# Overflow rows of a mixture of experts: from a scatter through memory to a product with a slot-by-token table

## What is computed

```
scores = sigmoid(x @ router_w)            # 16 experts in 4 groups
g_best = the best group; idx = the 2 best experts in it
gates  = scores of these two, divided by their sum
a   = einsum('td,edf->tef', x, w_gate);  up = einsum('td,edf->tef', x, w_up)
mid = silu(a) * up * gates
y   = einsum('tef,efd->td', mid, w_down)
x   = x + gate_vector * y                 # adaLN gate, one vector for prompt, one for sample
```

## Time and profile before

| what | us |
|---|---|
| median of three runs (range) | 875.19 (871.82 to 876.34) |
| the profiled execution | 876.51 |
| its span, first to last instruction | 874.6 |
| PE / DVE / ACT / POOL busy | 791.7 / 359.8 / 284.9 / 109.2 |
| mean granted TensorE clock | 0.965 of 2.4 GHz |

### The profile page before, as it was taken

One profiled execution on the slowest core, in us unless ns is written; L12 is line 12 of the kernel. 1 busy time (PEld: TensorE's weight loads), 2 busy tenths in 40 slices (PEclk: granted clock), 3 DMA queues, 4 the chain that ended last, 5 costly groups with the idle time before them and its releaser, 6 DMA issues.

```text
span 874.6 us, 11923 instructions
## 1 busy us (share of the span) xinstructions
PE 791.7 (91%) x4251; PEld 455.1 (52%) x4251; DVE 359.8 (41%) x837; ACT 284.9 (33%) x663; POOL 109.2 (12%) x155
## 2 busy tenths in 40 slices
PE   7999999999899999999885889999999999999860
PEld 4358755535444566555444536656544575554430
DVE  5770642642463442422115364475632434221115
ACT  1651222201640341222213347677611422221111
POOL 1400000010000011110112021320300111110120
PEclk8999999999899989999998899999999999999995
DMA  8993333299943387999987964320156669999955
GB/s 280 368 346 105 102 103 116 88 348 300 341 170 124 107 319 255 409 410 409 410 326 254 368 234 156 99 65 35 51 173 260 225 196 403 411 410 409 400 200 216
DMA packets 84119, 218.67 MB, mean 250 GB/s; under 512 B 9682, under 2 KB 19547, under 8 KB 83741
## 3 DMA queue, kind: packets, MB, share of 16 engines
q1 hardware_dynamic: 74046, 197.89, 62.1%
q0 software_dynamic: 8512, 16.48, 5.4%
q10 hardware_dynamic: 1504, 3.56, 1.1%
HBM read 213.13 MB, written 14.83 MB: 261 GB/s over the span
## 4 chain that ended last, share of the span: by engine, by line
PE 54%; DMA 11%; SPq 11%; issue 10%; DVE 6%; ACT 3%; POOLq 3%; DVEq 1%; POOL 1%; ACTq 0%
PE ps L980 49%; SPq L722 4%; SPq L692 4%; DMA arena<-in_moe_w_up_dram 3%; PE ps L987 3%; DMA ring<-in_moe_w_down_dram 2%; DMA hT_xn<-y_rows 2%; SPq L675 2%; DMA x<-in_x_sample_dram 2%; SPq L728 1%; DMA mod_rows<-modrow 1%; PE ps L1222 1%; DVEq L2068 1%; POOLq L948 1%; DMA y_rows<-arena,rows_in 1%
## 5 line engine op out<-in xcount | busy, mean ns | idle before, releaser
L980 PE MATMUL ps<-arena 128*64 128x256 f32 (+12 forms) x1164 | 222.2, 428 | 13.6 <-DMA arena<-in_moe_w_up_dram 6.3
L980 PEld LDWEIGHTS ps<-arena 128*64 128x64 f32 (+3 forms) x1164 | 121.0, 158 | 95.4 <-issue 51.3
L980 PE MATMUL ps<-ring,hT_xn 128*128 128x512 f32 (+2 forms) x384 | 134.6, 512 | 4.5 <-issue 3.9
L980 PEld LDWEIGHTS ps<-ring,hT_xn 128*128 128x128 f32 x384 | 73.8, 193 | 63.3 <-issue 58.9
L980 PE MATMUL ps<-ring,arena 128*64 128x256 f32 (+1 forms) x624 | 89.7, 433 | 6.9 <-DMA ring<-in_moe_w_up_dram 3.6
L1696 ACT ACTIVATE arena<-ps 128x256 f32<-128x256 f32 (+4 forms) x94 | 42.3, 463 | 86.1 <-PE ps L980 84.0
L980 PEld LDWEIGHTS ps<-ring,arena 128*64 128x64 f32 x624 | 42.9, 137 | 43.7 <-issue 23.1
L980 PE MATMUL ps<-hT_xn,ring 128*128 128x384 f32 x192 | 62.1, 486 | 0.0
L2485 DVE TENSOR_TENSOR arena<-arena,ps 128x128 f32<-128x128 f32 x37 | 10.7, 288 | 122.2 <-ACT arena L1823 122.2
L980 PE MATMUL ps<-hT_xn,arena 128*64 128x256 f32 (+3 forms) x340 | 58.1, 427 | 1.9 <-DVE hT_xn L2164 1.7
L987 PE MATMUL ps<-ident,arena 128*128 128x128 f32 (+2 forms) x332 | 49.2, 283 | 7.3 <-DVE arena L2790 1.4
(11 more groups left out here) (310 smaller groups left out, 890.6 us busy)
## 6 DMA issues: line engine op xcount, KB each, us to landing
ring<-in_w_mod_dram SPq DMA_DIRECT2D x48, 1024.0 KB, 8.5
arena<-in_moe_w_gate_dram SPq DMA_DIRECT2D x36, 512.0 KB, 13.1
arena<-in_moe_w_up_dram SPq DMA_DIRECT2D x36, 512.0 KB, 14.9
ring<-in_moe_w_down_dram SPq DMA_DIRECT2D x18, 1024.0 KB, 18.2
ring<-in_moe_w_gate_dram SPq DMA_DIRECT2D x30, 512.0 KB, 14.6
ring<-in_moe_w_up_dram SPq DMA_DIRECT2D x30, 512.0 KB, 16.9
arena<-in_moe_w_down_dram SPq DMA_DIRECT2D x20, 512.0 KB, 15.0
ring<-in_ev_w_in_dram SPq DMA_DIRECT2D x9, 1024.0 KB, 12.1
```

The source lines that it names most:

```text
L980: mm = pe.matmul(out, lhsT, rhs, **kw)
```

## The change

- **Result of an overflow block.** DVE multiplies the block's output by the adaLN gate twice, once by the prompt's and once by the sample's vector (`gate_halves`), into `ysb`, whose 128 partitions hold the left columns of the 64 rows in the upper half and the right columns in the lower half. ACT no longer takes part, and nothing is scattered.
- **The table.** For each block DVE makes `token_table`, 128 partitions by 384 tokens: the routing gate where the slot's token is this column, zero elsewhere (`token_ids`, `place_gate`; the tables are set up in the main loop at e = 8, and the plan at e = 4 and 6 grows by a few operations; on PE by a second group of six products of 22 columns).
- **The sums.** `over_sums`: six products per block, for three tiles by two column halves, each over 64 rows of `token_table` and 512 columns of `ysb`, into six banks. DVE adds the six banks to `x` (`add_over`). In the loop the sums and adds of block b - 1 stand in block b; those of the last block stand behind the loop, and `x_done` is signalled by the adds.
- **Order on PE.** `turn_in` of block b moves from block b - 1 to the head of block b, behind the `down` of the block before and ahead of the sums. The second `over_free` is signalled by `down`.
- **Rows back.** All six transfers are issued by ACT, behind block 0 and before the loop, after both `y_stored` semaphores show all main scatters landed.
- **Rows that main blocks don't write.** `y_rows` is filled once with the input rows (`start_rows`, four transfers of memory to memory from SP in the Hyena stage), and `gates_main` is zero where a token's row is in an overflow block.
- Between the layers PE makes 14 products instead of 28 to keep busy; SP waits for `over_done` instead of `y_back` before it loads the latent weights.

The diff, cut to its core:

```diff
+            def over_tables(l):
+                for t in range(NT):
+                    dve.tensor_scalar(token_ids[:, P * t:P * t + P], slots, float(P * t), None, ALU.add)
...
+            def add_over(l, t, count, banks, done):
+
+                dve.wait_ge(over_sum[l], count)
+                for half in range(2):
+                    part = x[:, t, HY * half:HY * half + HY]
+                    ins = dve.tensor_tensor(part, part, ps[banks[t][half]][:, :], ALU.add)
+                ins.then_inc(done, 1)
...
+                def over_sums(banks):
+
+                    for t in range(NT):
+                        for half in range(2):
+                            rows = slice(HALF * half, HALF * half + HALF)
+                            mm = product(ps[banks[t][half]][:, :], token_table[rows, P * t:P * t + P], ysb[rows, 0, HY * GRP[t]:HY * GRP[t] + HY], start=True, stop=True)
+                        mm.then_inc(over_sum[l], 1)
+
                 def over_block(b, slots):
                     looped = slots is OVER_SLOT
-                    for half in range(2):
-                        pe.wait_ge(xt_read[half][l], b + (NPAIR + 1))
+                    if looped:
+                        pe.wait_ge(over_gathered[l], b * 16 + 16)
+                        pe.wait_ge(over_added[l], b * NT)
+                        turn_in(xg_over, None)
+                        pe.wait_ge(y_read[0][l], NE + 1)
+                        pe.wait_ge(over_done[l], b)
+                        for half in range(2):
+                            pe.wait_ge(xt_read[half][l], b + (NPAIR + 1))
+                        over_sums(SUM_BANKS)
...
-                    pe.wait_ge(over_gathered[l], b * 16 + 32)
-                    turn_in(xg_over, None, over_free[l] if looped else None)
...
+                for parity in range(2):
+                    act.wait_ge(y_stored[parity][l], 16 * (NPAIR // 2))
+                for t in range(NT):
+                    act.dma_start(y_first[t], y_rows[P * t:P * t + P, :]).then_inc(y_back[t], 16)
+                    act.dma_start(y_second[t], y_rows[T + P * t:T + P * t + P, :]).then_inc(y_back[t], 16)
                 nb = blocks_of(act, l)
                 with act.Fori(1, nb) as b:
-                    over_block(b, over_done)
-                act.wait_ge(y_stored[1][l], 16 * (NPAIR // 2 - 1))
-                act.wait_ge(over_gathered[l], nb * 16 + 32)
-                act.wait_ge(over_stored[l], nb * 16 + 16)
-                for t in range(NT):
-                    act.dma_start(y_of[0][:, t, :], y_rows[P * t:P * t + P, :]).then_inc(y_back[t], 16)
+                    over_block(b, True)
...
+                    for g, done in enumerate((y_read[1], over_done if looped else y_read[0])):
+                        dve.tensor_tensor(ysb[:, 0, HY * g:HY * g + HY], ps[Y_BANKS[0]][:, :], gate_halves[:, g, :], ALU.mult).then_inc(done[l], 1)
```

More of the change, by code:

```diff
@@ L533, in build_step @@
         htok = xn
-        y_of = [xn, view(7680, NT, D)]
         spare = flat_hT.rearrange("p (a b) -> p a b", b=D)
+        y_first = [xn[:, t, :] for t in range(NT)]
+        y_second = [spare[:, 2, :], spare[:, 1, :], view(D, D)]
+        gate_halves = view(5120, 2, HY)
+        token_ids, token_table = view(6464, T), view(6848, T)
         xg = [spare[:, c % 2, :] for c in range(NPAIR)]
@@ L769, in _ @@
                 if i == at["in1.1"] + 1:
-                    rows_back(0, nb)
-                    for t in range(NT):
-                        sp.wait_ge(y_back[t], 32)
+                    sp.wait_ge(over_done[0], nb)
                     for j in range(2):
@@ L1222, in turn_in @@
                             mm = pe.transpose(ps[XT_BANKS[half]][:, q * P:(q + 1) * P], src[:, (4 * half + q) * P:(4 * half + q + 1) * P], ident[:, :])
-                            if gate_up_done is not None and half == q == 0:
-                                mm.then_inc(gate_up_done, 1)
                         mm.then_inc(xt_full[half][l], 1)
@@ L1324, in experts @@
                         bank = ps[MT_BANKS[0]]
-                        pe.wait_ge(over_hit[l], 1)
-                        for i in range(2 * NT):
-                            mm = product(bank[0:HALF, 256:256 + 2 * NOVER], hit_over[:, i, :], row_table[:, 2 * NOVER * i:2 * NOVER * i + 2 * NOVER], start=i == 0, stop=i == 2 * NT - 1)
-                        mm.then_inc(over_idx[l], 1)
+                        pe.wait_ge(over_hit, l + 1)
+                        for half in range(2):
+                            for i in range(2 * NT):
+                                mm = product(bank[HALF * half:HALF * half + HALF, 256:256 + 2 * NOVER], hit_over[:, i, :], row_table[:, 2 * NOVER * i:2 * NOVER * i + 2 * NOVER],
+                                             start=i == 0, stop=i == 2 * NT - 1)
+                        mm.then_inc(over_idx, 1)
                 main_mid(NE - 1)
@@ L1608, in _ @@
             moe(0)
-            for half in range(2):
-                pe.wait_ge(y_read[half][0], NE)
-            for _ in range(28):
-                product(ps[Y_BANKS[1]][:, 0:2 * P], ident[:, :], rowsel[:, :, :].rearrange("p a b -> p (a b)"), start=True, stop=True)
+            for _ in range(14):
+                product(ps[XT_BANKS[1]][:, 0:2 * P], ident[:, :], rowsel[:, :, :].rearrange("p a b -> p (a b)"), start=True, stop=True)
             mixer_turn(1, 0)
@@ L1860, in experts, with over_block @@
                 main_result(NE - 1)
-                def over_block(b, done):
+                def over_block(b, looped):
+                    if looped:
+                        act.wait_ge(xt_full[0][l], b + (NPAIR + 1))
+                        rows_copy(xgT[:, 0, 0:4, 0:HALF], HALF)
                     act.wait_ge(gu_full[l], b + (NE + 1))
@@ L2476, in over_lists @@
-                dve.drain().then_inc(over_rows[l], 1)
+                dve.tensor_scalar(place_gate[:, :, 0], ps[MT_BANKS[0]][:, 256:256 + NOVER], float(NO_ROW), None, ALU.add)
+                dve.tensor_copy(place_gate[:, :, 1], ps[MT_BANKS[0]][:, 256 + NOVER:256 + 2 * NOVER])
+                dve.drain().then_inc(over_rows, 1)
                 dve.tensor_copy(row_now[:, :], rows_over[:, 1:2]).then_inc(row_ready[l], 1)
+            def over_tables(l):
+                for t in range(NT):
+                    dve.tensor_scalar(token_ids[:, P * t:P * t + P], slots, float(P * t), None, ALU.add)
+                for h2 in range(2):
+                    for c in range(2):
+                        drained_wait(dve, f"modsel{l}.{G2}.{h2}", c)
+                for half in range(2):
+                    rows = slice(HALF * half, HALF * half + HALF)
+                    dve.tensor_copy(gate_halves[rows, :, :], gb[rows, :, HY * half:HY * half + HY])
@@ L2521, in experts, with over_block @@
                         over_lists(l)
+                    if e == 8:
+                        over_tables(l)
                 main_result(NE - 1)
-                def over_block(b):
+                def over_block(b, looped):
+                    if looped:
+                        dve.wait_ge(xt_full[1][l], b + (NPAIR + 1))
+                        rows_copy(xgT[:, 0, 4:8, 0:HALF], HALF)
+                        dve.tensor_copy(row_now[:, :], rows_over[:, bass.ds(b + 1, 1)]).then_inc(row_ready[l], 1)
+                        for t in range(NT):
+                            add_over(l, t, b * NT + t, SUM_BANKS, over_added[l])
                     dve.wait_ge(silu_ready[l], b + (NE + 1))
```

145 lines of the change are left out of this document (66 added, 79 removed).

## The result

| kernel | median us (range) | span of the profiled run | ratio to before (95% interval) |
|---|---|---|---|
| before | 875.10 (871.82 to 876.34) | 874.6 | 1 |
| after | 883.44 (881.25 to 885.23) | 883.4 | 1.010 (1.0064 to 1.0136) |

The changed kernel is slower by 1.0%. I had put 60% on no difference within 0.5% and 28% on slower; the time is 7.1 us over the forecast and inside the range, 0.6 us from its upper end.

The account below looks back on a forecast made before the run. TensorE carried 54% of the chain, DMA and SyncE's queue 22%; the change rewrites two serial stretches. Layer 0 gains 3.0 us, layer 1 loses 4.1: +1.1 on the median 875.19 gives 876.3 us, range 869 to 884.

Parts of the forecast that it names:

- Part 1: Block's result kept on chip: two VectorE products cost 1.4 us on the path; table and slot's gate cost nothing.
- Part 2: Six products of sums per block: 3.2 us a set, ends 2.6 and 5.2, on the path in the looped blocks.
- clock rival: Rival: TensorE's clock stays up through the first latent projection, taking 3.1 us off; chance 0.10.
- Part 4: Rows back early: ScalarE's six issues (2.7 us), loop entry (0.3) and copy (0.4) delay block 1's sums to 451.6 and 835.0.
- Part 3: Rows turned at the head of each looped block: sums start 1.9 us after the output; last block's gather wait removed.
- Part 5: The fill of `y_rows`, the additional plan products and the sooner load of latent weights: all three cost nothing.
- The tails: Behind each layer's last output: no wait for rows, joins at a pitch of 5.45 us; layer 1's tail gains 5.0 us.
- the halves don't overlap: Rival: the sums' half-array products run one after the other, 5.2 us a set, +6.0 us, 882.3 us; chance 0.12.
- ScalarE's queue: Rival: ScalarE's issues at 1.07 us delay block 1's sums by 3.8 us a layer, +7.5, 883.8 us; chance 0.16.
- Hides in the wait: Rival: inserted work in the looped blocks hides in waits for weights, leaving only shorter tails, 864.0 us; chance 0.07.
- The clock stays up: Rival: TensorE's clock holds into the first latent projection, 3.1 us off; with fully parallel sums 871.3 us; chance 0.10.
- a set of sums over 4.3 us: Sign of being wrong: a block's six sum products on TensorE take over 4.3 us, where about 3.2 was forecast.

Follow-up runs that it names:

- Run 3: The changed kernel with eight more products, results unread, on TensorE between block 0 and the loop; ScalarE keeps its six issues: 878.62 us, ratio 1.003.
- run 4: The changed kernel with ScalarE issuing the six row transfers behind its loop instead of ahead of it: 879.53 us, ratio 1.0028.
- run 6: The changed kernel with every product of the loop's sums done twice, result unchanged: 890.70 us, ratio 1.0172.
- run 8: The changed kernel with the six row transfers on SyncE behind its weight-request loop, plus ten more TensorE products ahead of the latent projection: 868.93 us, ratio 0.9918.
- runs 1 and 2: The changed kernel with GpSimd issuing the six row transfers, 899.29 us; the same with the loop's sums behind the gate and up products, 899.96 us.

## Why the prediction was off by 7 us, step by step

The ledger, on the profiled executions (predicted span 875.7, measured 883.4):

| stretch | predicted | measured | off |
|---|---|---|---|
| to the end of block 0's output, layer 0 | 447.8 | 447.2 | -0.6 |
| to block 1's output | 14.3 | 17.9 | +3.6 |
| to the latent projection | 17.7 | 18.0 | +0.3 |
| to block 0's output, layer 1 | 348.2 | 349.8 | +1.6 |
| to block 2's output | 26.8 | 29.7 | +2.9 |
| to the span's end | 20.8 | 20.9 | +0.1 |

The rows are rounded; the whole is 7.7 us.

- **Part 1** held: two products of 1.29 us together, 1.4 expected, and the table hidden.
- **Part 2**, the sums: at full clock a pair of instructions on half the rows each takes 0.43 us, the time of one instruction on all rows. That is 2.6 us for six pairs and 2.8 for the stretch that a set takes, near the lower end; I took 3.2 from the single pair of the earlier trace rows. The term that I did not have is the clock: 5.0 and 5.3 us in the two first looped blocks. I had a clock rival, and the earlier trace rows show what a wait does to the next products, but I applied it only to the latent projection and not to the wait that my own Part 4 put ahead of the sums. That is the step that failed. From the start of the sums to the block's output it took 12.4 and 12.8 us there and 10.1 in block 2, where I had 10.5: +1.9 in layer 0, +2.3 and -0.4 in layer 1. Run 3 shows it: with the queue left as it is and the clock held, 4.8 us come back. The Trainium skill (TensorEngine Tiling (Array Packing), Tiling Modes, Key Properties) lets tiles run in parallel, which the 0.43 us a pair confirms. The drain that it names for a change of mode is at most the 0.2 us between the last pair and the next load; nothing here tells it from the end of a group.
- **Part 3** held: behind a block with nothing else in ScalarE's queue the sums start 1.8 us after the output (852.38 behind 850.57).
- **Part 4** had the right mechanism and the wrong size. Six issues took 3.6 us in layer 0 and 3.0 in layer 1, not 2.7, and the loop's entry 1.0, not 0.3: the sums started 5.4 and 5.0 us behind block 0's output, not 3.8 and 3.9. By my numbers TensorE would have stood idle for some 2.8 us behind its transposes (448.8 to 451.6); it stood 4.4 and 4.0. So this size may also have had a hand in the clock: in run 4 the transposes between the layers came after 2.5 us of idle time and still had a granted clock of 1.00, and ahead of the sums no trace has a wait between 1.4 and 3.8 us. That no weight would be late was right.
- **Part 5** held, as far as the scatter of the stretch between the layers lets one say.
- **The tails** held to 0.3 us: the pitch of the joins is 5.5 us (864.01 to 869.51), the rows were back, the projection still began at the lower clock (8.3 us).
- Of the **rivals**, "the halves don't overlap" came out near the truth in price (5.2 a set) and wrong in cause. "ScalarE's queue" has part of the truth, 1.0 to 1.6 us a layer, far from 3.8. "Hides in the wait" is refuted by run 6 (and its price was wrong: the 12.3 us come off before's 875.2, not off the forecast, which makes 862.9 and not 864.0). "The clock stays up" did not happen by itself; run 8 made it happen, and it gave 2 us, not 3.1.
- Of the **signs of being wrong**, one came true, a set of sums over 4.3 us, in two sets of three; of ScalarE's issues only one took 1 us (1.02, the last of layer 0). That the time is inside the range all the same is luck in part: the range reached up to 884 for rivals that are not the cause.

What the stretch between the layers had from the change stays open: 1.6 us of the 7.7 may be no more than chance, though both traces of after are at the high end and both dip at 626 to 640 us.

## What to carry over

A DMA issue is not free for the engine that makes it: count its length, the entry of the loop or the drain behind it, and who waits for the first real instruction after it, and put it in the queue where nobody does. When a change puts a wait ahead of products, price those products at the clock that such a wait leaves, not at the clock of the busy stage where their duration was read. A 1% loss was here a good change in the wrong queue: moving six issues made 883 us into 871.

## What the runs showed of the hardware

- After standing idle for 3.8 to 4.4 us (six waits in the traces of the changed kernel and of run 6) TensorE began the sums at the lower level of its clock (granted clock 0.58 and 0.51 in the windows above); after 0.8 and 1.4 us it did not (1.00). Eight products whose results nobody reads made the kernel 5 us faster. The Trainium skill (TensorE: Matmul & The Clock Gate, Part 1: The HAM clock gate) says that the throttled clock is the resting state and that activity releases it; runs 3 and 8 agree.
- Six transfers of 512 KB cost ScalarE 2.8 to 3.9 us (single issues from 0.35 to 1.08), SyncE 2.8 us in layer 0 and 4.1 in layer 1 (0.34 to 1.13), and GpSimd 3.2 us and then a drain of 13.6 to 15.0 us, which ended 1.0 us after the last of them had landed, in all four cases of runs 1 and 2.
- Two instructions on the two halves of the rows take no longer together than one on all rows: 0.43 us for 512 columns each at full clock, 0.85 at the lower level.
